# Weight halves requested on ScalarE's queue, and key transposes ahead of the lower weight part, in a hybrid decoder step

## The reference, cut to what matters

```python
h = rmsnorm(x, g_pre1) * (1.0 + sc1) + sh1
proj = jnp.dot(h, w_in)
hq, hf, hi, hg, aq, ak, av, ua, ub = jnp.split(proj, splits, axis=-1)
...
k_past = cache_k[l][page_table].reshape(bs, n_pages * PAGE_SIZE, AT_HEADS, AT_DH)
...
kmean = jnp.mean(kb.astype(jnp.float32), axis=2)
gate = jnp.einsum('bhqd,bnhd->bhqn', qh, kmean)
_, sel = lax.top_k(gate, ksel)
...
s_sel = jnp.einsum('bhqd,bhqkld->bhqkl', qh, k_sel)
```

## Time and profile before

| | us |
|---|---|
| median of 3 runs | 751.43 |
| lowest and highest | 750.09, 752.02 |
| profiled execution | 755.44 |
| its span | 753.6 |
| PE busy | 641.5 (85%) |
| VectorE busy | 414.8 (55%) |
| ScalarE busy | 274.6 (36%) |
| GpSimd busy | 74.8 (10%) |
| DMA, mean over the span | 224 GB/s |

### The profile page before, as it was taken

The page is one execution under the profiler, slowest core; times in us unless marked ns, Lnnn a source line. Parts: engine busy times, 40 slices in busy tenths (PEclk is TensorE's granted clock), DMA queues, the critical chain, the costliest instruction groups (busy, mean ns, idle before and its releaser), DMA issues.

```text
span 753.6 us, 13191 instructions
## 1 busy us (share of the span) xinstructions
PE 641.5 (85%) x5260; PEld 539.9 (72%) x5260; DVE 414.8 (55%) x529; ACT 274.6 (36%) x388; POOL 74.8 (10%) x82
## 2 busy tenths in 40 slices
PE   4678998678888878968987599955999999999995
PEld 1275997657777767933332299935999999999993
DVE  0751577676666875755862247476453535341526
ACT  1432434342233433525132223343454545332412
POOL 2140010042333600000000000003000000000000
PEclk9979999999899998989699689987999999999998
DMA  9969834878677786689999977700555555747501
GB/s 334 413 253 349 305 105 134 272 247 275 224 239 260 256 266 217 219 278 346 311 306 341 364 265 227 255 1 4 166 166 167 167 167 167 278 138 254 168 1 63
DMA packets 98007, 168.98 MB, mean 224 GB/s; under 512 B 7121, under 2 KB 38537, under 8 KB 95778
## 3 DMA queue, kind: packets, MB, share of 16 engines
q1 hardware_dynamic: 92082, 162.86, 64.1%
q10 hardware_dynamic: 5152, 3.08, 1.3%
q0 software_dynamic: 720, 2.32, 0.8%
HBM read 163.51 MB, written 4.72 MB: 223 GB/s over the span
## 4 chain that ended last, share of the span: by engine, by line
PE 59%; DVE 19%; DMA 7%; issue 5%; SPq 5%; ACT 4%; POOL 1%; ACTq 0%; DVEq 0%
PE ps L1310 15%; PE ps L1312 15%; PE ps L1311 15%; DVE KT L994 6%; DMA ring<-w_in 4%; SPq L361 3%; ACT w_hi L553 2%; PE ps L1465 2%; DMA ring<-cache_v 2%; DVE w_lo L865 2%; PE ps L1328 1%; DMA ring<-w_ada 1%; SPq L327 1%; PE ps L1486 1%; PE ps L1472 1%
## 5 line engine op out<-in xcount | busy, mean ns | idle before, releaser
L865 DVE TENSOR_TENSOR w_lo<-ring,w_hi 128x1024 fp32r<-128x1024 f32 (+1 forms) x128 | 156.0, 1237 | 154.9 <-ACT w_hi L553 154.3
L1310 PE MATMUL ps<-h_hi,w_hi 128*128 128x288 f32 x704 | 216.2, 307 | 21.9 <-DVE w_lo L865 12.0
L1311 PE MATMUL ps<-h_lo,w_hi 128*128 128x288 f32 x704 | 211.4, 300 | 0.0
L1312 PE MATMUL ps<-h_hi,w_lo 128*128 128x288 f32 x704 | 210.6, 299 | 0.0
L553 ACT ACTIVATE w_hi<-ring 128x1024 fp32r<-128x1024 f32 (+1 forms) x128 | 131.5, 1042 | 161.6 <-PE ps L1312 71.6
L1310 PEld LDWEIGHTS ps<-h_hi,w_hi 128*128 128x128 f32 x704 | 136.1, 193 | 26.4 <-DVE w_lo L865 13.1
L1311 PEld LDWEIGHTS ps<-h_lo,w_hi 128*128 128x128 f32 x704 | 136.1, 193 | 0.6 <-issue 0.5
L1312 PEld LDWEIGHTS ps<-h_hi,w_lo 128*128 128x128 f32 x704 | 136.1, 193 | 0.0
L994 DVE STREAM_TRANSPOSE KT<-ring 128x1024 f32<-128x1024 f32 x64 | 75.0, 1217 | 0.9 <-DMA ring<-cache_k 0.8
L1465 PE MATMUL ps<-KT,Wk 128*32 128x128 f32 x1024 | 38.1, 294 | 34.5 <-DVE KT L994 34.0
L1465 PEld LDWEIGHTS ps<-KT,Wk 128*32 128x32 f32 x1024 | 28.7, 117 | 43.9 <-DVE KT L994 32.4
(11 more groups left out here) (294 smaller groups left out, 834.8 us busy)
## 6 DMA issues: line engine op xcount, KB each, us to landing
ring<-cache_k SPq DMA_DIRECT2D x128, 256.0 KB, 3.6
ring<-cache_v SPq DMA_DIRECT2D x128, 256.0 KB, 4.0
ring<-w_ada SPq DMA_DIRECT2D x24, 1024.0 KB, 10.2
ring<-w_in SPq DMA_DIRECT2D x44, 512.0 KB, 5.8
ring<-w_gu SPq DMA_DIRECT2D x44, 512.0 KB, 4.8
ring<-w_down SPq DMA_DIRECT2D x20, 512.0 KB, 4.5
ring<-w_out SPq DMA_DIRECT2D x8, 512.0 KB, 5.9
S<-state_hgrn SPq DMA_DIRECT2D x4, 512.0 KB, 6.1
```

Of the source, the lines that this page charges most:

```text
L865: dve.tensor_tensor(w_lo[:, s, k, :], slot4(s)[:, k, :], w_hi[:, par, k, :].bitcast(F32), ALU.subtract).then_inc(sem("lo_split"), 1)
L1310: pe.matmul(dst, h, x_hi, start=first, stop=False)
L1311: pe.matmul(dst, h, x_lo, start=False, stop=False)
L1312: return pe.matmul(dst, l, x_hi, start=False, stop=last)
```

## The change

The requests of 21 weight halves, from block 10's first to block 20's first, leave SP's list and are written into ScalarE's instructions: in each step but the first, ScalarE waits for `w_used` and requests the half three further on, ahead of its `w_hi` of that step. And in VectorE's steps the transposes of the step's units now stand ahead of `w_lo`, the score sums behind it.

```diff
+    BESIDE = [("w", n // 2, n % 2) for n in range(2 * FUSED[0] + 4, 2 * FUSED[-1] + 5)]
...
+    def fetch_half(engine, n):
+
+        w, half = n // 2, n % 2
+        engine.wait_ge(sem("w_used"), n - 3)
+        engine.dma_start(slot4(SLOT["w", w])[:, 2 * half:2 * half + 2, :],
+                         w_src("w_in", ((w % 2) * BK + 2 * half) * P, GROUP[w // 2] * BC, rows=2 * P)).then_inc(sem(landed("w", w, half)[0]), 16)
...
             looped = LOADS.index(("gu", 36, None))
             for n in range(looped):
+                if LOADS[n] in BESIDE:
+                    continue
...
             for w in FUSED:
                 for half in range(2):
+                    if w > FUSED[0] or half == 1:
+                        fetch_half(act, 2 * w + half + 3)
                     hi_wh(w + 1, half)
...
             for w in FUSED:
                 for half in range(2):
+                    for u in units(w, half):
+                        turn_keys(u)
                     lo_wh(w + 1, half)
                     for u in units(w, half):
-                        turn_keys(u)
                         if u % 4 == 0 and u >= 8:
                             block_sums(u // 4 - 2)
```

## The result

| | before | after |
|---|---|---|
| median of 4 executions | 751.72 us (750.09 to 753.11) | 718.28 us (717.19 to 724.07) |
| the profiled execution | 755.44 us, span 753.6 | 717.96 us, span 716.1 |

The ratio is 0.957 with a 95% interval of 0.952 to 0.963. The change wins 33.4 us. The profiled execution of before was 3.7 us above its median, so differences between the two traces come out some 4 us larger than those between the medians. Among the executions of the kernel before that the experiments were timed beside, one of 829.3 us with a granted clock of 0.725 is left out.

What follows compares the result with a forecast made beforehand. PE's 34 us of waits for transposes, late because VectorE waits for w_hi, were taken as the bound; 11 us would remain (3 first units, 8 second), so 23 come off the 751.43 us median: 728.4 us, range 719 to 741.

Steps and rivals of the forecast that it cites:

- What bounds: Stretch from 118 to 303 us: PE waits 34.0 us for transposes, late because VectorE waits for w_hi before w_lo.
- The first units: PE's waits before each step's first unit, 22.5 us, go except 0.4 us in eight steps behind a merge, 3 us.
- The second units: PE's waits before the second unit of ten steps, 11.5 us, shrink to 8 us, limited by when pages land.
- Step (12, 0): The step worked out as example, projection from 182.98 us: of PE's 4.72 us of waits, 0.7 to 0.8 remains.
- The clock: PE's granted clock, 0.59 between 190 and 198 us: fewer waits should give back 0 to 4 us, left out.
- Longer landing: Pages land later as DMA moves 278 GB/s in the stretch: worth 0 to 4 us, left out against the clock.
- The transfers: Rival: pages can't be drawn faster than about 260 GB/s, the stretch needs 173 us; 739 us, chance 0.08.
- The weights' room: Weight halves have 2 us to spare; rival: landing past 7.4 us makes w_lo wait, 740 us, chance 0.06.
- the slower case: Rival: two queues share the DMA engines; decisive from landings of 8.1 us, 780 us at 9.9; chance 0.05.
- The queue edit alone: Weight requests moved to ScalarE's queue without VectorE's new order: worth about nothing, between -5 and +3 us.
- the signs listed: New profile: KT wait 6 to 16 us, w_hi under 20, some page waits, near 280 GB/s, weight landing under 7.

Runs made afterwards that it cites:

- keys_first_only: The kernel before with only VectorE's order changed (transposes first, w_lo second, score sums last), all weight requests still on SP: 717.65 us, ratio 0.950.
- half_pages: VectorE's order alone, with only the first half of each key page's columns loaded from unit 2 on: 710.04 us, ratio 0.940.
- request_last: The kernel after, with ScalarE's weight request moved from ahead of the step's w_hi to the step's end, behind its score copies: 750.68 us, ratio 0.994.
- weight_ahead: VectorE's order alone, with each weight half put ahead of its step's key pages in SP's list: 750.15 us, ratio 0.993.
- queue_only: The kernel after with VectorE's old order put back, the weight halves still requested on ScalarE's queue: 749.52 us, ratio 0.991.
- full_again: The kernel after, unaltered, timed once more on the same chip as its separate halves: 722.28 us, ratio 0.954.
- numbers_first: The kernel after, with SP reading a load's page numbers before it waits for the slot: 715.28 us, ratio 0.948.

## Why the prediction was right, and where it missed

**What bounds.** Right. The wait for w_hi was the cause of the late transposes: with the order alone it fell from 53.2 to 7.7 us and the time by 5.0% (keys_first_only).

**The first units** (22.5 us to 3). Near in size: 4.8 us remain, in waits before 150 us. The reason given was not theirs: pages stood behind two of them and the recurrence's scans behind the largest, as the rows above show. The steps behind a merge were to keep 0.4 us each, and PE's waits for the transposes show none there. But PE waits for the merges themselves, hA, 3.0 us (2.5 of them in the row of waits above), and it waited 2.4 before, so this is no loss.

**The second units** (11.5 us to 8). Mis-sized: 3.7 us remain. The step that failed is the one in which the second unit's last page "is asked for at about 183.3". That time was read from the trace of before, where SP stood 75.5 us for the very transposes that now come earlier. SP now stands 53.5 us for them, and the requests move forward with them. Step (12, 0), worked out as an example, did keep the 0.7 to 0.8 us forecast for it (0.79), and was then taken for ten steps when it is the only one after 150 us. Even in that step the match is luck. SP's last two requests for the unit's pages, the landing of the last, and the last transpose:

```profile
169.73 0.85 SPq L369 DMA_DIRECT2D ring<-cache_k  x2
```
```profile
DMA to landing us min/median/max: 5.5/5.5/5.5
```
```profile
175.81 1.25 DVE L1006 STREAM_TRANSPOSE KT<-ring 128x1024 f32<-128x1024 f32 x1
```

The last page was asked for at about 170.2, 1.7 us before the step's projection began at 171.9; the prediction had it 0.3 us behind that. Then it took 5.5 us to land, not 3.8. The two errors cancel. And the transposes before it started 1.15 us apart, by which the last could have begun at 175.6: the page held it up by 0.2 us, the rest of the 0.79 is VectorE's, which came from the merge only at 172.2.

**The clock** (0 to 4 us, left out). The largest miss: 9 us. PE was busy 148.0 us before and 139.0 after, for the same matmuls. The granted clock allows for that: 6% missing of 185 us are 11 us, 1% of 150.4 are 1.5, so by this estimate up to some 10 us of PE's work could come back. Two groups of matmuls in this stretch, first before, then after (line, operation, count, busy us, mean ns of one, idle before):

```profile
L1465 PE MATMUL ps<-KT,Wk 128*32 128x128 f32 x1024 | 38.1, 294 | 34.5 <-DVE KT L994 34.0
L1542 PE MATMUL ps<-hvtok,hktok 128*128 128x128 f32 x16 | 3.6, 412 | 0.0
```
```profile
L1478 PE MATMUL ps<-KT,Wk 128*32 128x128 f32 x1024 | 34.2, 278 | 8.4 <-DVE KT L1006 8.4
L1555 PE MATMUL ps<-hvtok,hktok 128*128 128x128 f32 x16 | 2.1, 281 | 0.0
```

The key matmuls went from 38.1 to 34.2 us, and the product in the second rows, with no wait of its own, from 3.6 to 2.1. The prediction had one half-speed stretch in view (0.59 from 190 to 198 us) and took it for a single case. In the trace of before eight further slices of 8 us stand at 0.95 or less; in that of after there is one:

```profile
133.00:141.00 8.00, 5.35 (x89) 4.72 (x88) 5.67 (x6) 2.74 (x5) 1.21 (x2) 1.00 0.91 309
141.00:149.00 8.00, 5.41 (x79) 4.74 (x82) 8.00 (x10) 1.50 (x3) 2.71 (x3) 1.00 0.70 252
149.00:157.00 8.00, 8.00 (x86) 5.85 (x78) 8.00 (x10) 4.31 (x5) 1.38 (x2) 0.79 0.92 295
```

PE was busy for 5.35 and 5.41 us of the two slices ahead of it; in no later slice was it busy for less than 7.15, and the clock stayed at 1.00.

The stretch fell by 34.6 us, 25.6 of it idle time of PE and 9.0 busy time. The 23 forecast were idle time alone, so the forecast missed 2.6 us of waits and all of the 9.0. That fewer waits raise the clock is read from when it fell and rose; no run here changed the clock with the waits left alone.

**Longer landing** (0 to 4 us, left out as cancelling the clock). Key pages land in a median of 4.5 us for 3.8, and still the waits fell more than forecast. The two terms were set against each other by their size, not by any row that tied them, and they did not cancel.

**The transfers.** Rightly ranked low. The stretch draws 295 GB/s, and 303 from 150 us on; a limit of 260 isn't there. But half_pages shows that pages cost most of what is left above PE's own work: without half of their bytes the time was 9.6 us shorter.

**The weights' room** and **the slower case.** The weights land in a median of 6.0 us (5.3 before), inside the bound of 7.4, the slowest in 7.8, and PE's waits hold none for w_lo. request_last shows how near the edge lay. The slower case needed landings of 8.1 us for the key pages; the slowest was 7.4.

**The queue edit alone** (-5 to +3). At the edge of the forecast: 6.3 us won, 4 to 10 by the interval. Beside VectorE's order no gain can be seen, which the prediction didn't separate from its worth alone. The Trainium skill's "DMA: Bandwidth & Descriptors", section "Issuing engines are not separate DMA queues", agrees with that second result: it grants a second issuing engine only the time to start a DMA. The prediction's further reading, that position in SP's order would then be worth nothing, is refuted by weight_ahead with 30 us.

**Of the signs listed**, PE's wait for KT (8.4 us; 6 to 16), VectorE's for w_hi (5.3; under 20), waits for pages (12.0), the requests on ScalarE's queue (0.37; about 0.4) and their landing (6.0; under 7) came as said, and no wait of PE for w_lo came; the rate, 295, is above the 280 named, as the stretch was shorter.

## What to carry to other kernels

In an engine that works in order, put first what its consumer needs next, and behind it what is needed a step later: here one moved call was worth 5%, and 28 to 31 us were lost again when a request stood behind a wait that ends later than its own, on SP's queue or on ScalarE's. When costing waits that vanish, move the requests that were waiting for the same event along with them, and count TensorE's clock: in these traces 15 to 26 us more of scattered waits came with 9 to 12 us more of busy time. Ask of a second queue not whether it is faster but what each request stands behind.

## What the runs showed of the hardware

PE's busy time for the same work, about 1,790 recorded matmuls, falls into two groups over the kernels of this study. Where the granted clock of the stretch was 0.96 to 0.99 it was 138 to 142 us; in the four with 0.91 to 0.94 (before, queue_only, request_last, weight_ahead) 148 to 151. The full level is 2.4 GHz and the other 1.2, so part of each second group's stretch ran at the lower one. Those four have 30 to 37 us of PE idle there, the ten others 4 to 16. Within a group the busy time does not follow the idle time: keys_first_only has 141.6 us busy with 9.2 idle, full_again 139.1 with 14.9.

With 0.88 to 0.90 of DMA time taken and 295 to 303 GB/s, against 0.76 and 243 before, key pages took a median of 4.5 us for 3.8 and weight halves 6.0 for 5.3. Asked for on SP's queue alone, at 294 GB/s, they took 4.1 and 5.7: of the 0.7 us, 0.3 to 0.4 came with a fifth more bytes per us. Counted without the eight pages of values at the stretch's end, and beside VectorE's new order, the three kernels with two queues (the kernel after, full_again, numbers_first) had pages at 4.5 to 4.6 us and halves at 6.0 to 6.5, the three comparable ones with one queue 4.1 to 4.2 and 5.7 to 5.8, at 288 to 302 GB/s. In the old order, at 247 GB/s, the second queue made no such difference: 3.7 and 5.4 us in queue_only, 3.7 and 5.3 before. What in the new order adds the 0.2 to 0.8 us is not shown.
